# Expert slots of 64 rows in 16 rounds, or of 32 rows in 12 fixed passes: an encoder trunk with a sparse expert layer

## The chip, the cores and the metric

The kernel runs on one core of a Trainium2 chip. The time is the device time of one execution in microseconds, the median of several.

## The reference

Two layers work on 528 real positions (16 learned meta tokens and 512 frames) of 1024 features in float32. Layer 0 is multi-scale retention and then an expert layer; layer 1 is sliding-window attention with sinks and then an expert layer; a final norm follows. The diff touches only the expert layers:

```python
g_sel = argmax(softmax(t @ w_group))              # one of 4 groups
top_p, top_i = top_k(softmax(logits of the 4 experts in that group), 2)
weights = g_w * top_p / sum(top_p)
expert_idx = g_sel * 4 + top_i                    # 2 of 16 experts for each token
a, u = t @ w_gate[e], t @ w_up[e]                 # 1024 -> 256, each
y += (silu(a) * u * gate) @ w_down[e]             # 256 -> 1024
```

Gate and up weights of one expert are 2 MB, down weights 1 MB. Layer 0 routes 528 tokens, layer 1 512 (the meta tokens' outputs are no longer needed), each to two experts.

## The kernel before, in words

**Order of the stages.** Retention (up to about 540 us), expert layer 0, key/value/query projections and attention, expert layer 1, final norm. Each engine has its program written out by hand, with semaphores; nothing is planned by a scheduler. SP (SyncE) issues the loads of weights known beforehand, ACT (ScalarE) those of rows and the stores of results, POOL (GpSimd) the indirect transfers.

**Routing (DVE, L1436 to L1466).** PE's logits and a matmul with a triangular matrix give each token its rank within its expert. Each expert has a slot block of BLK = 64 rows; what is beyond is put into overflow blocks, of which there can be 16. DVE computes the slot of each token (`slot_i`, semaphore `slot_ready`) and then, for each overflow block, the rows of its expert's weights in DRAM (`w_row`, `eb_ready`). POOL scatters the normed tokens to `slot_rows` in DRAM (L1696, two transfers for a tile of tokens, ten in layer 0, eight in layer 1).

**Rounds.** A round works on 128 slot rows, two blocks of 64, each with its own expert. ACT loads the rows (`load_rows`, L1116), PE transposes them (L814, bank B_ROWS), DVE copies them with the gain, PE multiplies with gate and up weights (L828: 8 chunks of features, two halves of 64 columns, into one PSUM bank at partitions 0 and 64), ACT and DVE make the hidden values, PE transposes these (L835) and multiplies with the down weights (L849, banks B_YA and B_YB), ACT and DVE copy the result, ACT stores it to `slot_out`. PE's order is written out: gate/up k, hidden k-1, rows k+1, down k-1, then gate/up k+1. There are 8 rounds for the 16 experts' own blocks and 8 for the overflow blocks, whatever the routing.

**Weights.** Four buffers (`gu`, `down`) hold the weights of four blocks, so of two rounds. `first_weights` loads the first four during the stage before. SP's `experts` (L605) reloads the two buffers of round k when gate/up k-2 is done, and their down halves when down k-2 is done. From round 8 on POOL's `spilled` (L1700) does the same by indirect DMA, with the row indices from `w_row`: indices beyond a bound are skipped, so an unused overflow block loads only partition 0. POOL works this list strictly in order, waiting at each step.

**After the rounds** POOL gathers each token's two results (L1718) and DVE adds them, weighted, to the residual.

Of the kernel before, what the change touches and what calls it, by code (L numbers as in the profile page):

```python
# [32 lines left out]
BLK = 64  # L33
RING = 3
SLOTS_W = 4


def most_overflow(tokens):

    return max(m + min(m * ((tokens - BLK - 1) // BLK), (2 * tokens - (BLK + 1) * m) // BLK)  # L40
               for m in range(1, EXPERTS + 1) if (BLK + 1) * m <= 2 * tokens)


OVER = most_overflow(POS)
assert OVER % SLOTS_W == 0 == EXPERTS % SLOTS_W
THRESH = (POS - 1) // BLK
ROUNDS = (EXPERTS + OVER) // 2
SLOTS = 2 * ROUNDS * BLK
assert (EXPERTS + OVER) % 2 == 0 and ROUNDS % 2 == 0 and most_overflow(SEQ) <= OVER


C_ID, C_ONE, C_512, C_TRI = 0, 128, 256, 384
C_REV, C_THR, C_VALID, C_NH, C_EPS, C_FIRST, C_OVER, C_BLK, C_CAP, C_ROW = (
    512, 516, 524, 529, 534, 535, 551, 567, 583, 584)
NCONST = 586
# [4 lines left out]
def tables():  # L60
# [8 lines left out]
    c[:, C_THR:C_THR + THRESH] = np.arange(1, THRESH + 1) * BLK  # L69
    c[:, C_FIRST:C_FIRST + EXPERTS] = np.arange(EXPERTS) * BLK  # L70
    c[:, C_OVER:C_OVER + EXPERTS] = EXPERTS - 1 - np.arange(EXPERTS)
    c[:, C_BLK:C_BLK + OVER] = np.arange(OVER)
    c[:, C_CAP] = EXPERTS
    c[0, C_CAP] = EXPERTS - 1
# [106 lines left out]
def build(nc, a, out):  # L181
# [4 lines left out]
    with ctx:  # L186
# [21 lines left out]
        w_row = sb("w_row", [128, 2, OVER], I)  # L208
# [82 lines left out]
        down = cv(SLOTS_W, 2, D)  # L291
        gu_3 = cv(KT * 512)
        xg = cv(2, D)
        xgT = cv(2, KT, 128)
# [3 lines left out]
        lg = cv(5, 20)  # L298
        small = cv(1300)
        next_junk = cv(D)  # L300
        moe_junk = [arena[:, VALUES + KT * 512:VALUES + KT * 512 + D], arena[:, 15360:15360 + D]]
# [26 lines left out]
        slot_out = nc.dram_tensor("slot_out", (SLOTS, D), F).ap()  # L328
# [81 lines left out]
        def sigs(names, tag):  # L410
# [8 lines left out]
        gu_in, down_in, gu_over, down_over = ([sem(f"{n}{s}") for s in range(SLOTS_W)] for n in (  # L419
            "gate_up_in", "down_in", "gate_up_overflow_in", "down_overflow_in"))  # L420
# [10 lines left out]
        def gu(k):  # L431

            return gu_3 if k % SLOTS_W == 3 else ring[:, (k % SLOTS_W + 1) % RING]

# [5 lines left out]
        def weights_arrived(eng, given, spilled, l, k):  # L440

            if k < EXPERTS:
                eng.wait_ge(given[k % SLOTS_W], 16 * ((l * EXPERTS + k) // SLOTS_W + 1))
            else:
                eng.wait_ge(spilled[k % SLOTS_W], 16 * ((l * OVER + k - EXPERTS) // SLOTS_W + 1))

# [42 lines left out]
        sizes = dict(MASK=80, OV=80, T1=5, TOP=5, EQ=20, OHG=20, EG=20, G44=80, SEL=20, M1=5, M2=5, OH1=20, OH2=20, DX=5,  # L489
                     MA=80, MB=80, W1=5, W2=5, PRE=96, C5=16 * THRESH, NB=16, Z16=16, INCL=16, EB=16 * OVER, EBS=OVER,  # L490
                     BASE=16, SL=80, SF=10)
        ends = np.cumsum([0] + list(sizes.values())).tolist()
        (_, OV, T1, TOP, EQ, OHG, EG, G44, SEL, M1, M2, OH1, OH2, DX, MA, MB, W1, W2, PRE, C5, NB, Z16, INCL, EB, EBS,
         BASE, SL, SF) = ends[:-1]
# [6 lines left out]
        def gu_bank(k):  # L501
            return 2 + k % 2
# [13 lines left out]
        def in_pair(k):  # L516

            return 16 * (k // 2 + 1)
# [32 lines left out]
        def _(sp):  # L551
# [35 lines left out]
            def gate_up_weights(l, k):  # L587
                sp.dma_start(gu(k), a["w_gu"][l, k]).then_inc(gu_in[k % SLOTS_W], 16)

            def down_weights(l, k):  # L590
                sp.dma_start(flat(down[:, k % SLOTS_W]), a["w_down"][l, k])\
                    .then_inc(down_in[k % SLOTS_W], 16)

            def first_weights(l, readers):

                for k, used in enumerate(readers):
                    used()
                    gate_up_weights(l, k)
                    if k == 2:
                        down_weights(l, 0)  # L600
                        down_weights(l, 1)
                down_weights(l, 2)
                down_weights(l, 3)
# [10 lines left out]
            first_weights(0, (lambda: out_chunk_used(sp, 2), lambda: None,  # L614
                              lambda: out_chunk_used(sp, 3), lambda: None))
# [9 lines left out]
            for c in range(2):  # L625
# [5 lines left out]
                              lambda: fl.wait_full(sp, f"WO{NT - 1}"), lambda: None))  # L631
# [11 lines left out]
        def _(pe):  # L643
# [145 lines left out]
            def experts(l):  # L789
# [28 lines left out]
                def gate_up(k):  # L818
                    b = gu_bank(k)
                    for g in range(2):  # L820
                        weights_arrived(pe, gu_in, gu_over, l, 2 * k + g)
                    round_read(pe, l, B_ROWS, k)
                    if k >= 2:
                        round_read(pe, l, b, k - 2)
                    for c in range(KT):
                        for g in range(2):
# [12 lines left out]
                def down_project(k):  # L839
                    for g in range(2):  # L840
                        weights_arrived(pe, down_in, down_over, l, 2 * k + g)
                    round_read(pe, l, B_HID, k)
                    for n, b in enumerate((B_YA, B_YB)):
                        if k:
                            round_read(pe, l, b, k - 1)
                        for c in range(2):
                            for g in range(2):
                                half = slice(BLK * g, BLK * g + BLK)
                                last = mm(ps[half, b, :], hidT[:, c, half],  # L849
                                          down[:, (2 * k + g) % SLOTS_W, c, 512 * n:512 * n + 512],  # L850
                                          start=(c == 0), stop=(c == 1))
# [128 lines left out]
        def _(act):  # L980
# [114 lines left out]
            def experts(l, ready):  # L1095
# [15 lines left out]
                def load_rows(k):  # L1111

                    if k < ROUNDS:
                        if k >= 2:
                            round_full(act, l, B_ROWS, k - 2)
                        act.dma_start(xg[:, k % 2, :], slot_rows.rearrange("(b p) c -> b p c", p=2 * BLK)[k])\  # L1116
                            .then_inc(m[f"x_in{k % 2}"], 16)
# [5 lines left out]
                def results_of(k):  # L1123
# [3 lines left out]
                    if k >= 2:  # L1127
# [4 lines left out]
                    act.dma_start(slot_out.rearrange("(b p) c -> b p c", p=2 * BLK)[k], yo[:, j, :])\  # L1132
                        .then_inc(m[f"y_out{j}"], 16)
# [65 lines left out]
        def _(dve):  # L1199
# [158 lines left out]
            def experts(l):  # L1358
# [77 lines left out]
                step(V_.tensor_tensor(v(C5, 16, THRESH), count.unsqueeze(2).to_broadcast([128, 16, THRESH]),  # L1436
                                      con[:, C_THR:C_THR + THRESH].unsqueeze(1).to_broadcast([128, 16, THRESH]),
                                      ALU.is_gt))
                step(V_.tensor_reduce(v(NB, 16), v(C5, 16, THRESH), X, ALU.add))
                step(V_.memset(v(Z16, 16), 0.0))  # L1440
                step(V_.tensor_tensor_scan(v(INCL, 16), v(NB, 16), v(Z16, 16), 0.0, ALU.add, ALU.add))

                first = con[:, C_FIRST:C_FIRST + 16].unsqueeze(1).to_broadcast([128, nt, 16])
                step(V_.tensor_tensor(v(BASE, 16), v(INCL, 16), v(NB, 16), ALU.subtract))
                step(V_.tensor_tensor(v(BASE, 16), v(BASE, 16), con[:, C_OVER:C_OVER + 16], ALU.add))
                step(V_.tensor_scalar(v(BASE, 16), v(BASE, 16), float(BLK), None, ALU.mult))
                sl, over = v(SL, nt, 16), v(OV, nt, 16)
                V_.tensor_tensor(sl, ps[:, 2, 0:16 * nt].rearrange("p (t e) -> p t e", e=16), before[:, 0:nt, :],
                                 ALU.add).then_inc(free[2], 1)
                fl.wait_read(dve, f"RK{l}")  # L1450
                step(V_.scalar_tensor_tensor(over, sl, BLK - 0.5, v(BASE, 16).unsqueeze(1).to_broadcast([128, nt, 16]),
                                             ALU.is_gt, ALU.mult))
                step(V_.tensor_tensor(sl, sl, first, ALU.add))
                step(V_.tensor_tensor(sl, sl, over, ALU.add))
                for n, at in enumerate((MA, MB)):
                    step(V_.tensor_tensor(v(at, nt, 16), v(at, nt, 16), sl, ALU.mult))
                    step(V_.tensor_reduce(v(SF, 2, 5)[:, n, 0:nt], v(at, nt, 16), X, ALU.add))
                V_.tensor_copy(slot_i[:, :, 0:nt], v(SF, 2, 5)[:, :, 0:nt]).then_inc(m["slot_ready"], 1)
# [339 lines left out]
```

## Time and profile before

| | us |
|---|---|
| median of 3 runs | 1501.71 (1496.98 to 1505.82) |
| the profiled execution | 1498.73 |
| its span, first to last instruction | 1496.6 |
| PE busy | 1175.5 (79%) |
| PE weight loads (beside the matmuls) | 727.3 (49%) |
| DVE busy | 454.4 (30%) |
| POOL busy | 302.2 (20%) |
| ACT busy | 242.8 (16%) |
| mean granted TensorE clock | 0.888 |

Busy shares are means over stages with different limits. PE is nearly always busy during retention; in the two expert layers the DMA queues are the busiest for about half of each, and PE waits. The chain of waits and the instructions in order of time tell which it is at each place.

### The profile page before, as it was taken

How to read it: one execution, taken by the hardware profiler on the slowest of the kernel's cores; microseconds unless marked ns; L12 is line 12 of the kernel's file. 1: busy time of each engine (PE TensorE's matmuls, PEld its weight loads, DVE VectorE, ACT ScalarE, POOL GpSimd, SP SyncE). 2: the span in 40 equal slices, each digit the busy share in tenths (PEclk: the TensorE clock that was granted, in tenths of full speed). 3: DMA queues.
4: the chain of work that ended last, by engine and by line, in shares of the span. 5: the costliest groups of instructions: out<-in, count | busy, mean ns of one | idle time of the engine just before them, and what ended most of it. 6: DMA issues, size and time to landing. Idle time of an engine off the chain costs nothing.

```text
span 1496.6 us, 14033 instructions
## 1 busy us (share of the span) xinstructions
PE 1175.5 (79%) x5748; PEld 727.3 (49%) x5748; DVE 454.4 (30%) x736; ACT 242.8 (16%) x451; POOL 302.2 (20%) x232
## 2 busy tenths in 40 slices
PE   5999999999989982777779649688868296777790
PEld 4789698897967771322223224343434232322230
DVE  4212234322581033211112162635544311111114
ACT  4122221321421110000001010213213000000011
POOL 4133132231532202000222242100000200012124
PEclk9999999999999975988889959898988588998895
DMA  6141221321302353899995163100201769999825
GB/s 241 42 155 58 83 101 56 129 68 56 141 1 94 131 225 144 328 414 424 386 397 188 67 262 133 42 0 0 77 36 63 289 237 414 427 384 403 338 74 196
DMA packets 47176, 273.32 MB, mean 183 GB/s; under 512 B 8742, under 2 KB 8870, under 8 KB 33270
## 3 DMA queue, kind: packets, MB, share of 16 engines
q1 hardware_dynamic: 21168, 151.26, 25.7%
q0 software_dynamic: 13952, 77.15, 13.0%
q10 hardware_dynamic: 12000, 44.12, 7.4%
q8 instruction: 41, 0.67, 0.2%
q14 instruction: 15, 0.12, 0.0%
HBM read 277.28 MB, written 35.78 MB: 209 GB/s over the span
## 4 chain that ended last, share of the span: by engine, by line
PE 58%; issue 15%; DVE 11%; DMA 7%; POOL 6%; ACT 2%; ACTq 0%; POOLq 0%; SPq 0%; DVEq 0%
PE ps L665 19%; PE ps L828 14%; PE ps L849 6%; PE ps L886 4%; PE ps L972 4%; POOL ring_r L1672 4%; DMA ring<-in_w_gu,w_row 3%; PE ps L877 3%; DMA ring<-in_w_gu 2%; PE ps L814 2%; PE ps L798 2%; PE ps L751 2%; POOL slot_rows L1696 1%; DVE xT L1218 1%; DVE arena L1599 1%
## 5 line engine op out<-in xcount | busy, mean ns | idle before, releaser
L828 PE MATMUL ps<-ring,arena 128*64 128x512 f32 x768 | 258.4, 657 | 105.5 <-issue 99.5
L828 PEld LDWEIGHTS ps<-ring,arena 128*64 128x64 f32 x768 | 81.7, 151 | 272.9 <-issue 272.9
L665 PE MATMUL ps<-x_hi,ring_r 128*128 128x264 f32 x1024 | 190.9, 287 | 7.0 <-DVE xT_r L1206 7.0
L1672 POOL TENSOR_TENSOR ring_r<-ring,ring_r 128x1024 fp32r<-128x1024 f32 x56 | 134.2, 2408 | 301.5 <-ACT ring_r L999 301.5
L1218 DVE TENSOR_TENSOR arena<-ps,gains 128x512 f32<-128x512 f32 (+1 forms) x74 | 46.7, 673 | 397.8 <-PE ps L814 384.1
L665 PE MATMUL ps<-ring_r,x_hi 128*128 128x512 f32 (+1 forms) x480 | 155.8, 406 | 11.6 <-POOL ring_r L1672 11.6
L665 PEld LDWEIGHTS ps<-x_hi,ring_r 128*128 128x128 f32 x1024 | 160.3, 189 | 7.5 <-DVE xT_r L1206 7.3
L665 PE MATMUL ps<-xT_r,ring_r 128*128 128x264 f32 x512 | 146.1, 285 | 0.0
L828 PE MATMUL ps<-arena 128*64 128x512 f32 x256 | 133.9, 683 | 0.0
L849 PE MATMUL ps<-arena 128*64 128x512 f32 x512 | 116.9, 598 | 4.3 <-ACT arena L1121 4.3
L665 PEld LDWEIGHTS ps<-ring_r,x_hi 128*128 128x128 f32 (+1 forms) x480 | 84.3, 176 | 43.3 <-POOL ring_r L1672 13.1
L665 PEld LDWEIGHTS ps<-xT_r,ring_r 128*128 128x128 f32 x512 | 97.0, 189 | 0.1
L999 ACT ACTIVATE ring_r<-ring 128x1024 fp32r<-128x1024 f32 x56 | 57.7, 1052 | 123.1 <-PE ps L665 73.7
L1121 ACT ACTIVATE arena<-ps 128x256 f32<-128x256 f32 x32 | 12.3, 383 | 388.3 <-PE ps L835 383.8
L1702 POOL DMA_INDIRECT arena<-in_w_down,w_row x32 | 31.6, 988 | 202.7 <-PE ps L849 197.8
L1702 POOL DMA_INDIRECT ring<-in_w_gu,w_row x24 | 23.9, 995 | 240.7 <-PE ps L828 234.0
L814 PE MATMUL ps<-con,arena 128*128 128x128 f32 x256 | 35.1, 283 | 46.3 <-DMA arena<-slot_rows 46.3
L886 PE MATMUL ps<-ring,xT 128*128 128x512 f32 x128 | 59.8, 628 | 10.2 <-DVE arena L1599 10.2
L849 PEld LDWEIGHTS ps<-arena 128*64 128x64 f32 x512 | 34.7, 136 | 64.0 <-issue 64.0
L665 PE MATMUL ps<-ring_r,xT_r 128*128 128x512 f32 (+1 forms) x160 | 65.0, 406 | 0.0
L1660 POOL TENSOR_SCALAR var<-ss 128x1 f32<-128x1 f32 (+1 forms) x23 | 9.0, 391 | 259.8 <-ACT arena L987 259.3
L653 PE MATMUL ps<-con,arena 128*128 128x128 f32 (+1 forms) x152 | 24.1, 320 | 41.1 <-DVE arena L1212 39.3
(177 smaller groups left out, 1494.9 us busy)
## 6 DMA issues: line engine op xcount, KB each, us to landing
ring<-in_w_gu SPq DMA_DIRECT2D x24, 2048.0 KB, 14.1
arena<-in_w_down SPq DMA_DIRECT2D x32, 1024.0 KB, 10.4
ring<-in_w_ret SPq DMA_DIRECT2D x48, 512.0 KB, 3.6
arena<-in_w_gu SPq DMA_DIRECT2D x8, 2048.0 KB, 19.1
arena<-slot_rows ACTq DMA_DIRECT2D x32, 512.0 KB, 7.3
slot_out<-arena ACTq DMA_DIRECT2D x32, 512.0 KB
slot_rows<-arena ACTq DMA_DIRECT2D x8, 1024.0 KB, 4.0
ring<-in_w_ret_out SPq DMA_DIRECT2D x16, 512.0 KB, 4.5
```

What stands on the lines that cost most here:

```text
L665: last = mm(dst, a_parts[x], b_parts[y], start=(start and n == 0), stop=(stop and n == 2))
L751: last = mm(ps[:, b + g, c - lo:HALF], v_tm[0:r, t, 128 * m:128 * m + 128], scores_of(t)[0:r, c - 128 * t:hi - 128 * t], start=(t == 0), s ...
L814: last = nc.tensor.transpose(ps[:, c // 4, 128 * (c % 4):128 * (c % 4) + 128], xg[:, k % 2, 128 * c:128 * c + 128], ident)
L828: last = mm(ps[half, b, :], xgT[:, k % 2, c, half], by_row(gu(2 * k + g))[:, c, :], start=(c == 0), stop=(c == KT - 1))
L849: last = mm(ps[half, b, :], hidT[:, c, half], down[:, (2 * k + g) % SLOTS_W, c, 512 * n:512 * n + 512], start=(c == 0), stop=(c == 1))
L877: last = mm(ps[0:rows(t), b, :], xTk[:, k, col0(t):col0(t) + rows(t)], w_kv[:, k, :], start=(k == 0), stop=(k == KT - 1))
L886: last = mm(ps[:, b, :], xT[:, k, col0(t):col0(t) + 128], w_q[c][:, k, :], start=(k == 0), stop=(k == KT - 1))
L972: last = mm(ps[:, 4 + c, :], oT1[:, k, :], w[:, k, :], start=(k == 0), stop=(k == KT - 1))
L999: nc.scalar.activation(w_hi[to][:, m], w_raw[slot][:, m], ACT.Copy).then_inc(hi_made, 1)
L1218: return V_.tensor_tensor(dst[:, 4 * g:4 * g + 4, c0:c0 + r], src, gains[:, gain, 4 * g:4 * g + 4].unsqueeze(2).to_broadcast([128, 4, r]), ...
L1672: G.tensor_tensor(w_lo[slot][:, m], w_raw[slot][:, m], w_hi[to][:, m], ALU.subtract).then_inc(lo_made, 1)
L1702: return G.indirect_dma_start(dst, None, w.rearrange("l e p c -> (l e p) c"), bass.IndirectOffsetOnAxis(w_row[:, l, k - EXPERTS:k - EXPERT ...
```

## The change

Slots are counted in tiles of 32 rows. An expert with n tokens has ceil(n/32) tiles, taken two at a time as *pairs* (called doubles, "d", 64 rows) and the rest as *singles* ("s", 32 rows); there are 16 pair places and 16 single places. Single place j has no weights of its own: it shares the weight buffer of pair place j, and an expert's odd tile goes to the single beside its own pair where it has one. The passes are a fixed list of 12. A pass has 128 columns: two pairs, a pair and two singles, or four singles. With two singles in a half, gate/up and down have three matmuls for each chunk in place of two, with 64, 32 and 32 columns; with four singles, four.

The ring of weight buffers has six places (W_SLOTS). The first five experts are loaded ahead (AHEAD) in order of number. When the routing is known POOL goes over them (`others`, with `mended`) and loads another expert where the pair place has one; for the same expert all indices but that of partition 0 are out of bounds. From the sixth on SP loads with an address taken from the register of the expert's number. Before a pass with singles POOL goes over the two buffers once more (`reload`, with `gu_again` and `down_again`), which loads another expert if the single's is not the pair's, and only partition 0 if it is. PE waits for these in `weights_arrived`. Rows and results of a pass go in two transfers of 64 rows. DVE's routing is written anew.

```diff
-RING = 3
-SLOTS_W = 4
+TILE = 32
+W_SLOTS = 6
+AHEAD = 5
+PASSES = [(("d", 0), ("d", 1)), (("d", 2), ("s", 0)), (("d", 3), ("d", 4)), (("s", 2), ("d", 5)),
+          (("d", 6), ("s", 4)), (("d", 7), ("d", 8)), (("s", 6), ("d", 9)), (("d", 10), ("s", 8)),
+          (("d", 11), ("d", 12)), (("s", 10), ("d", 13)), (("d", 14), ("d", 15)), (("s", 12), ("s", 14))]
...
+        def column_tiles(k):
+            for n, (kind, j) in enumerate(PASSES[k]):
+                if kind == "d":
+                    yield slice(BLK * n, BLK * n + BLK), j
+                else:
+                    for g in range(2):
+                        yield slice(BLK * n + TILE * g, BLK * n + TILE * g + TILE), j + g
...
+        def weights_arrived(eng, first, again, l, k):
+            for kind, j in PASSES[k]:
+                if kind == "d":
+                    double_arrived(eng, first, l, j)
+                else:
+                    singles_arrived(eng, again, l, j)
...
             def experts(l):
-                for k in range(2, EXPERTS // 2):
-                    round_full(sp, l, gu_bank(k), k - 2)
-                    for g in range(2):
-                        gate_up_weights(l, 2 * k + g)
-                    round_full(sp, l, B_YB, k - 2)
-                    for g in range(2):
-                        down_weights(l, 2 * k + g)
+                m = mo[l]
+                sp.wait_ge(m["eb_ready"], 1)
+                for j in range(AHEAD, EXPERTS):
+                    if j < W_SLOTS:
+                        sp.wait_ge(m["scattered"], 16 * 2 * (5 - l))
+                    e = sp.value_load(e_of[0:1, l, j:j + 1], min_val=0, max_val=EXPERTS - 1)
+                    gu_d, dn_d = a["w_gu"][l], a["w_down"][l]
+                    if j >= W_SLOTS:
+                        round_full(sp, l, gu_bank(pass_of("s", j - W_SLOTS)), pass_of("s", j - W_SLOTS))
+                    gate_up_weights(l, j, gu_d[bass.ds(e, 1)].rearrange("a p c -> p (a c)"))
+                    if j >= W_SLOTS:
+                        round_full(sp, l, B_YB, pass_of("s", j - W_SLOTS))
+                    down_weights(l, j, dn_d[bass.ds(e, 1)].rearrange("a p c -> p (a c)"))
...
                     for c in range(KT):
-                        for g in range(2):
-                            half = slice(BLK * g, BLK * g + BLK)
-                            last = mm(ps[half, b, :], xgT[:, k % 2, c, half], by_row(gu(2 * k + g))[:, c, :],
+                        for cols, j in column_tiles(k):
+                            last = mm(ps[cols, b, :], xgT[:, k % 2, c, cols], by_row(gu(j))[:, c, :],
                                       start=(c == 0), stop=(c == KT - 1))
...
-                for k in range(EXPERTS // 2, ROUNDS):
-                    round_full(pool, l, gu_bank(k), k - 2)
-                    for n in (2 * k, 2 * k + 1):
-                        spilled(a["w_gu"], gu(n), n).then_inc(gu_over[n % SLOTS_W], 16)
-                    round_full(pool, l, B_YB, k - 2)
-                    for n in (2 * k, 2 * k + 1):
-                        spilled(a["w_down"], flat(down[:, n % SLOTS_W]), n).then_inc(down_over[n % SLOTS_W], 16)
+                for j in range(AHEAD):
+                    pool.wait_ge(gu_in[j % W_SLOTS], times_filled(l, j))
+                    others(a["w_gu"], gu(j), j).then_inc(mended[j // 2 > 0], 16)
+                    pool.wait_ge(down_in[j % W_SLOTS], times_filled(l, j))
+                    others(a["w_down"], flat(down[j % W_SLOTS]), j).then_inc(mended[j // 2 > 0], 16)
+
+                def reload(w, dst, arrived, k):
+                    for n in range(0, EXPERTS, 2):
+                        if pass_of("d", n + 1) == k:
+                            for j in (n, n + 1):
+                                others(w, dst(j), AHEAD + j).then_inc(arrived[n // 2 % 2], 16)
+
+                for k in range(ROUNDS):
+                    round_full(pool, l, gu_bank(k), k)
+                    reload(a["w_gu"], gu, gu_again, k)
+                    round_full(pool, l, B_YB, k)
+                    reload(a["w_down"], lambda j: flat(down[j % W_SLOTS]), down_again, k)
```

## Rows read from the trace of the kernel before

**Rows 1.** DMA rate (GB/s) in 40 slices of 8 us from 560 us.

```profile
GB/s 0 110 371 191 2 163 428 282 437 420 429 395 414 421 431 426 405 434 424 433 292 379 419 425 431 290 433 407 437 127 225 112 70 72 68 39 92 195 344 4
```

**Rows 2.** Chain that ended last, both expert stages (start us, us, what).

```profile
593.46 9.72 PE ps L828 x32
605.68 7.09 PE ps L828 x32
...
728.17 13.03 DMA ring<-in_w_gu,w_row
...
834.05 6.87 PE ps L828 x32
...
841.96 3.67 PE ps L849 x16
...
847.44 3.67 PE ps L849 x16
...
1201.36 9.56 PE ps L828 x32
...
1457.29 3.67 PE ps L849 x16
```

**Rows 3.** The page's DMA queues: packets, MB, share of 16 engines.

```profile
q0 software_dynamic: 13952, 77.15, 13.0%
```

**Rows 4.** PE in order of time, rounds of layer 0 (start us, us, line, operands [idle before]).

```profile
655.91 8.78 PE L828 MATMUL ps<-ring,arena 128*64 128x512 f32 x32 [3.01 <-issue]
795.31 3.65 PE L849 MATMUL ps<-arena 128*64 128x512 f32 x16
798.80 7.04 PE L828 MATMUL ps<-ring,arena 128*64 128x512 f32 x32
806.04 1.04 PE L814 MATMUL ps<-con,arena 128*128 128x128 f32 x8
807.01 3.65 PE L849 MATMUL ps<-arena 128*64 128x512 f32 x16
```

**Rows 5.** PE in order of time, single matmuls of L828.

```profile
606.57 0.59 PE L828 MATMUL ps<-ring,arena 128*64 128x512 f32 x1
606.60 0.59 PE L828 MATMUL ps<-arena 128*64 128x512 f32 x1
606.99 0.59 PE L828 MATMUL ps<-ring,arena 128*64 128x512 f32 x1
```

**Rows 6.** PE and its weight loads (PEld) at 453 us, L665.

```profile
453.05 0.39 PE L665 MATMUL ps<-ring_r,y_lo 128*16 128x512 f32 x1
453.27 0.39 PE L665 MATMUL ps<-w_hi_b,y_hi_b 128*128 128x512 f32 x1
453.05 0.19 PEld L665 LDWEIGHTS ps<-w_hi_b,y_hi_b 128*128 128x128 f32 x1
```

**Rows 7.** POOL in order of time, scatter and indirect loads.

```profile
583.36 0.84 POOL L1696 DMA_INDIRECT slot_rows<-arena,slot_i  x1 [0.30 <-issue]
799.77 0.99 POOL L1702 DMA_INDIRECT arena<-in_w_down,w_row  x1 [18.62 <-PE ps L849]
```

**Rows 8.** DMA issues: KB each, median us to landing; first 560 to 880, then 810 to 846.

```profile
arena<-slot_rows ACTq DMA_DIRECT2D x16, 512.0 KB, 7.3
...
arena<-slot_rows ACTq DMA_DIRECT2D x1, 512.0 KB, 3.3
...
ring<-in_w_gu,w_row POOLq DMA_INDIRECT x3, 3.1
```

**Rows 9.** DVE in order of time, routing of layer 0.

```profile
567.55 0.29 DVE L1436 TENSOR_TENSOR arena<-arena,con 128x128 f32<-128x128 f32 x1
...
570.02 0.24 DVE L1454 TENSOR_TENSOR arena<-arena 128x80 f32<-128x80 f32 x1
...
571.40 0.17 DVE L1458 CAST slot_i<-arena 128x10 int32<-128x10 f32 x1
571.48 0.42 DVE L1461 TENSOR_TENSOR arena<-arena,con 128x256 f32<-128x256 f32 x1
```

More of the change, by code:

```diff
@@ L290, in build @@
         cv = Carve()
[L291 to L294, printed above, removed]
+        gu_arena = cv(2, KT * 512)
+        down = [*(lambda d: [d[:, n] for n in range(AHEAD)])(cv(AHEAD, 2, D))]
         yo = cv(2, D)
@@ L846, in down_project @@
                         for c in range(2):
[L847 to L850, printed above, removed]
+                            for cols, j in column_tiles(k):
+                                last = mm(ps[cols, b, :], hidT[:, c, cols], down[j % W_SLOTS][:, c, 512 * n:512 * n + 512],
                                           start=(c == 0), stop=(c == 1))
@@ L1443, in experts @@
[L1443 to L1448, printed above, removed]
-                                 ALU.add).then_inc(free[2], 1)
@@ new lines, in experts @@
+                pos = v(POSN, nt, 16)
+                V_.tensor_tensor(pos, ps[:, 2, 0:16 * nt].rearrange("p (t e) -> p t e", e=16), before[:, 0:nt, :],
+                                 ALU.add).then_inc(free[2], 1)
+                step.done(V_.tensor_reduce(v(N_, 16), passed, X, ALU.add))
+                step.done(V_.memset(v(Z16, 16), 0.0))
+                step(V_.tensor_reduce(v(D_, 16), passed[:, :, 1:THRESH:2], X, ALU.add))
+                P0, P1 = v(PP, 17)[:, 0:16], v(PP, 17)[:, 1:17]
@@ new lines, in experts @@
+                step.done(V_.tensor_tensor(v(PC, nt, 16), pos, per_expert(v(CC, 16)), ALU.add))
+                step(V_.tensor_tensor(v(DBL, nt, 16), v(DBL, nt, 16), per_expert(v(CA, 16)), ALU.mult))
+                step(V_.tensor_tensor(v(PC, nt, 16), v(PC, nt, 16), v(DBL, nt, 16), ALU.add))
+                for at in (MA, MB):
+                    step.done(V_.tensor_tensor(v(at, nt, 16), v(at, nt, 16), v(PC, nt, 16), ALU.mult))
+                step.wait()
+                place = v(SLOT, 2, 5)
@@ new lines, in experts @@
+                step(V_.tensor_reduce(eo, match, X, ALU.add))
+                step.done(V_.tensor_scalar(v(FREE, 16), v(CL, 16), -1.0, 1.0, ALU.mult, ALU.add))
+                step(V_.tensor_scalar(eo, eo, float(EXPERTS - 1), None, ALU.min))
+                step.done(V_.tensor_copy(e_of[:, l, :], eo))
+                step.done(V_.tensor_copy(to[:, 0:AHEAD], eo[:, 0:AHEAD]))
+                step.done(V_.tensor_tensor(same[:, 0:AHEAD], eo[:, 0:AHEAD], num[:, 0:AHEAD], ALU.is_equal))
+                step.done(V_.tensor_tensor(dif, xo, num, ALU.add))
@@ new lines, in experts @@
+                step.wait()
+                step(V_.tensor_tensor(match, v(IL, 16).unsqueeze(1).to_broadcast([128, 16, 16]), c16(dif, 16), ALU.is_le))
+                step(V_.tensor_reduce(xo, match, X, ALU.add))
+                step.done(V_.tensor_tensor(dif, xo, eo, ALU.subtract))
+                step(V_.scalar_tensor_tensor(v(PM, 16), xo, float(EXPERTS), v(FREE, 16), ALU.is_lt, ALU.mult))
+                step(V_.tensor_tensor(dif, dif, v(PM, 16), ALU.mult))
+                step.done(V_.tensor_tensor(to[:, AHEAD:], eo, dif, ALU.add))
@@ L1468, in widen @@
+                step(V_.tensor_scalar(same[:, AHEAD:], dif, 0.0, None, ALU.is_equal))
+                step(V_.tensor_scalar(same, same, con[:, C_FAR:C_FAR + 1], con[:, C_ROW:C_ROW + 1], ALU.mult, ALU.add))
+                step(V_.scalar_tensor_tensor(to, to, 128.0, same, ALU.mult, ALU.add))
+                V_.tensor_scalar(w_row[:, l, :], to, float(128 * EXPERTS * l), None, ALU.add).then_inc(m["eb_ready"], 1)
                 def widen(k):
```

227 lines of the change are left out of this document (142 added, 85 removed).

## The prediction

> **What bounds the kernel now.** I read the page's busy shares first (PE 79%, nothing else over 30%), then its 40 slices, which show that DMA is nearly full only in the two expert stages, then the DMA rate inside them [rows 1], then the chain of waits in them [rows 2] and last the engines' own order of time. The reader is to see three phases in each expert stage (586 to 852 and 1194 to 1462 us). Rounds 2 to 7 wait for DMA: the ten slices from 632 to 712 us move 423 GB/s on average, and I take 420 for a full DMA [rows 1]. Rounds 8 to 12, the overflow rounds, wait for the indirect loads that POOL issues only when the round two before is done (the piece `ring<-in_w_gu,w_row` [rows 2]). Rounds 13 to 15 load next to nothing and run at PE's own pace. The expert part proper is 593.46 to 851.11 us in layer 0 and 1201.36 to 1460.96 in layer 1 (first L828 to the end of the last L849) [rows 2]: 257.7 and 259.6 us. Everything outside is a different stage that the diff leaves alone, but for the routing on DVE.
>
> **What the routing of this input is.** From the reference's inputs I counted the tokens of each expert: in both layers every expert has between 41 and 84, so each has one block of 64, and 9 of them in layer 0 and 10 in layer 1 one overflow block. The trace agrees: 19 spilled experts of 3.146 MB, 8.5 MB of scatter and 8.5 MB of gather, and row 0 of the 13 unused blocks make 77.1 MB, and q0 moved 77.15 [rows 3]. In the new scheme each expert therefore has one pair (j = e), and its third tile of 32, if any, is the single that shares its buffer. Nothing is mended or reloaded but partition 0. So the second load of 19 experts, 59.8 MB, goes; 142 us at 420 GB/s is an upper bound of what that alone could give. 16 rounds become 12 passes per layer.
>
> **PE's own time.** At full pace a round is 11.69 us: L828 starts at 798.80, L849 at 795.31 and again at 807.01, 11.70 later [rows 4]. An instruction streams 512 columns in 0.43 us, and the two halves of 64 columns run together: starts 0.03 us apart, the next two 0.43 later [rows 5]. A pass of two pairs is the same work. Six passes (1, 3, 4, 6, 7, 9) have a pair and two singles, three instructions in a step instead of two, and the last has four. A pass has 16 such steps in gate/up and 8 in down. The trace has no step of three tiles in different column groups. Bounds: 0.43 us, if all overlap (L814 and its loads issue 16 instructions in 1.04 us [rows 4], 0.065 each, so six loads and matmuls fit in 0.39); 0.86 us if tiles of 64 and of 32 columns take turns; 1.18 us, two whole instructions of 0.59, if the array also empties between them. I take 0.43: the nearest row is the change from 16 columns to 128 at 453 us, where the load for 128 starts with the last 16-column matmul (453.05) and its matmul 0.22 us later, the ordinary spacing, before the 0.39 of the last is over [rows 6]. There nothing empties. These two use the same columns, so the row doesn't show that different widths overlap; that stays the largest risk.
>
> The Trainium skill says the opposite for the emptying: "Mode switching requires drain", a change of tile shape drains TensorE (TensorEngine Tiling (Array Packing), Tiling Modes). By that rule the step is the 1.18 us case, and the trace disagrees with it for 16 against 128 columns. No row here shows it for 64 against 32.
>
> **The sum for one layer, first L828 to last L849.**
> Undisturbed: first to second L828 12.2 us (593.46 to 605.68), ten more passes of 11.69, and 17.0 from the last L828 to the end (834.05 to 851.11) [rows 2, 4]: 146.1.
>
> New waits. Every single's buffer now waits for an indirect load by POOL, though it carries only partition 0. POOL takes them strictly in order: gate/up of pass k, reload, *down of pass k*, reload. PE starts gate/up k+2 right after down k. So the reload of gate/up for a single in pass k+2 is issued only when down k has ended, with nothing of PE's left beside it. Price: POOL starts 0.81 us after down ends (798.96 to 799.77), the second load 1.29 later (0.99 and the 0.30 between two issues) [rows 4, 7], and a load of only row 0 lands 3.1 us after its issue where DMA is quiet [rows 8]: 5.2, and 5.4 with PE's head start of 0.16 (798.96 to 798.80). That is for passes 3, 6, 9. In passes 4, 7, 11 two down loads stand ahead on POOL, 2.6 more: 8.0. Pass 1 waits for the reload after gate/up 0: 603.18 + 0.8 + 1.29 + 3.1 = 608.4 against 605.7, 2.7. Down of the last pass waits for the reload behind down 10: 5.2 against a natural gap of 1.8 (845.6 to 847.44, [rows 2]), 3.4. Together 2.7 + 3 x 5.4 + 3 x 8.0 + 3.4 = 46.3.
>
> Contention. At passes 3, 6, 7 and 9 SP's weight loads are in flight. Row loads land in 7.3 us in the whole stage against 3.3 alone [rows 8]; twice as many bytes in time explains about one of the four, so I add 3 each, 12 (bounds 0 and 4 x 8).
>
> Clock. After an idle gap of 3.01 us the next gate/up took 8.78 us instead of 7.04 [rows 4], and after the long idle time before 593.46 9.72 [rows 2]: PE's clock stood at its lower level (1.2 GHz) for the first steps. The stalls here are a little longer than 3.01, so six at 1.9: 11.4.
>
> DMA as the limit. After the five experts loaded ahead 11 x 3.146 = 34.6 MB remain, with 12.6 MB of rows and results: 112 us at 420 GB/s. By buffers: the weights of 10 are issued after down 3, some 10 us behind those of 8 and 9, and are due at pass 7; those of 15 are issued after down 7, behind 12.6 MB since down 6, and land some 25 us after down 6, where pass 10 starts at 23.4 plus one stall. Everything is just in time, so I charge nothing.
>
> Loads and rows of the first passes: two experts' checks (four POOL issues, 5.2 us) follow the scatters and start at 583.36 + 0.84 + 0.3, the fourth at 588.4, and land at 591.5, before L828 at 593.5 [rows 7]: nothing. The six issues of the other three experts take 7.7 us more and land before pass 1. The fifth expert loaded ahead adds 3.1 MB, 7.5 us, to a queue that was empty before the scatter [rows 1]: nothing. SP's reading of the expert number stands before a wait that ends later: nothing.
>
> Routing on DVE. From L1436 to the end of L1458 4.0 us for 16 instructions; an instruction of 10 or 16 columns takes 0.17 us, of 80 0.24, of 256 0.42, and a dependent one starts 0.04 later [rows 9]. The new list up to slot_ready has 3.2 us of the first size (12 waits at 0.21, and what is issued between them at 0.08), 2.0 of 80 columns and 3.4 of 160 to 272: 8.6 us. +4.6, on the path, since the scatter waits for it. The list after it is longer, but lies beside 12.5 us of scatters.
>
> Stage: 146.1 + 46.3 + 12 + 11.4 = 215.8. Gains 257.7 - 215.8 - 4.6 = 37.3 and 259.6 - 215.8 - 4.6 = 39.2: 76.5. The profiled execution took 1498.7 (span 1496.6), 3.0 under the median 1501.7, so 1498.7 - 76.5 + 3.0 = 1425.
>
> **The rivals.**
> *A, the forecast*, 1425. Bounds within it: no contention and half the clock loss give 18 us a layer more, 1389; contention of 8 us at four passes 20 less, 1465.
> *B, the widths take turns, slower.* In a pair-and-singles pass steps of 64 and of 32 columns do not overlap: 0.43 us more in 24 steps of 6 passes, 62 us a layer. It decides from a step of 0.43 + 76.5/288 = 0.70 us on. For: [rows 5] show overlap only of equal widths. Against: [rows 6]. Time: 1425 + 124, less some 15 of contention that the slower pace removes, 1534.
> *C, they also empty the array.* 0.75 more, 216 in all: 1626. Against: [rows 6] again, and more plainly. This is what the Trainium skill's rule above would do here.
> *D, three tiles overlap, but the third adds its own issue*: L814's load and matmul take 0.13 us each (8 in 1.04 [rows 4]), a step 0.56: 288 x 0.13 = 37, 1462.
> *E, it doesn't do what it says*: experts are reloaded after all (another count in a tile at a threshold). 3.1 MB, 7.5 us at 420 GB/s, on the path per expert: two of them 1440. Against: the number of pairs changes only below 33 and above 96 tokens, and the counts are 41 to 84.
> *F, the waits on POOL are free*, if reloads land before PE needs them: 46 + 12 + 11 a layer less, 1287. Against: POOL's order.
>
> **Chances.** A 0.50, D 0.14, B 0.17, C 0.10, E 0.03, F 0.06. The range takes in A, D and B with their bounds and leaves out C and F: 1370 to 1550. Beside it, the likeliest's own: 1389 to 1465. About 0.5% (7.5 us) is what a measurement of this kernel tells from no change. Faster: A, D, E and F, less 0.02 for the upper end of D: 0.71. Same: those 0.02 and 0.01 of B's lower end. Slower: the rest of B, and C, 0.26.
>
> **What would show it.** L828's instructions in pass 3 start three together with 0.43 us between steps (B: 0.86, C: 1.18). Gate/up stands idle 5 to 12 us before passes 3, 4, 6, 7, 9, 11 and not before 2, 5, 8, 10, each time with a POOL load just ahead, not SP's. q0 moves about 18 MB, not 77. slot_ready comes 8 to 9 us after the compare. Wrong would be: gaps before passes 2, 5, 8 (then DMA is late), or busy time of L828 per pass over 9 us at full clock.

## The result and the profile after

The changed kernel takes 1704.8 us (median, 1700.1 to 1707.7) against 1501.7: ratio 1.135, 95% interval 1.130 to 1.140. It is 203 us slower where 77 us faster was forecast, and beyond the stated range.

| | before | after |
|---|---|---|
| profiled execution's span, us | 1496.6 | 1705.1 |
| q0 moved, MB | 77.15 | 18.12 |
| DMA packets under 512 B | 8742 | 16940 |
| first L828 (now L893) to last L849 (now L912), layer 0 | 257.7 | 348.1 |
| the same, layer 1 | 259.6 | 348.9 |

The bytes did what the prediction said. This is the page's queue after, for [rows 3]:

```profile
q0 software_dynamic: 16832, 18.12, 3.2%
```

The chain of waits in expert layer 0, after, for [rows 2] (start us, us, what; x48 is the gate/up of a pass with a pair and two singles, x32 of one with two pairs):

```profile
592.90 13.20 DMA arena<-in_w_down,w_row
606.35 9.94 PE ps L893 x32
618.35 3.51 DMA ring<-in_w_gu,w_row
622.10 17.52 PE ps L893 x48
...
644.45 6.87 PE ps L893 x32
652.56 7.96 PE ps L912 x24
662.64 12.90 DMA arena<-in_w_gu,w_row
675.58 18.20 PE ps L893 x48
695.02 3.58 PE ps L912 x16
698.61 8.76 issue
707.37 17.68 PE ps L893 x48
726.29 7.51 PE ps L912 x23
734.23 6.87 PE ps L893 x31
742.34 10.65 issue
753.00 10.77 PE ps L912 x24
...
944.28 3.74 DMA arena<-in_w_down,w_row
948.11 6.29 PE ps L912 x32
```

Two things are to be seen. A mixed gate/up takes 17.5 to 18.2 us where a plain one takes 6.87, and a mixed down 7.5 to 8.0 instead of 3.6: PE itself is slow. And PE stands idle before passes 3, 4 and down 4, for 15.1, 8.8 and 10.7 us. Ahead of pass 3 the chain names a load that carries `w_row`, so one of POOL's; ahead of pass 4 and down 4 it names no releaser ("issue"), and that these are POOL's loads too is shown only by e_noreload below. PE's waits for weights in this stage, grouped (us in total, times, longest):

```profile
PE ps L893 <- DMA arena<-in_w_gu,w_row: 30.0, 2, 15.1
PE ps L893 <- issue: 25.2, 3, 8.8
PE ps L912 <- issue: 21.2, 2, 10.7
PE ps L893 <- DMA ring<-in_w_gu,w_row: 20.1, 2, 15.3
PE ps L893 <- DMA arena<-in_w_down,w_row: 8.5, 1, 8.5
PE ps L912 <- DMA arena<-in_w_down,w_row: 5.5, 1, 5.5
```

That is 110.5 us, 102.0 of it after the first L893. PE in pass 4, in order of time, for [rows 5]:

```profile
716.06 1.05 PE L893 MATMUL ps<-arena,xT 128*32 128x512 f32 x4
717.04 1.07 PE L893 MATMUL ps<-ring,xT 128*64 128x512 f32 x2
718.04 1.05 PE L893 MATMUL ps<-arena,xT 128*32 128x512 f32 x4
```

A chunk has six instructions: the 64 column tile twice, one after the other, and then each of the two 32 column tiles twice, these two together. From 32 to 64 columns and back to 32 is 1.98 us (716.06 to 718.04). Four streams of 0.43 one after the other would be 1.72; so the widths do not overlap, and each of the two changes of width in a chunk costs 0.13. In pass 11, where all four tiles have 32 columns, they do overlap, all four within 0.02 us, and the next four start 0.43 later:

```profile
934.74 0.61 PE L893 MATMUL ps<-ring,xT 128*32 128x512 f32 x3
934.76 0.59 PE L893 MATMUL ps<-arena,xT 128*32 128x512 f32 x1
935.16 0.61 PE L893 MATMUL ps<-ring,xT 128*32 128x512 f32 x3
```

### The profile page after: what moved, and what is told of

It is laid out like the page before. It is cut to its first block, busy times and chain, and to the rows that moved or that the text cites. A ratio compares the mean times of both kernels' runs of the same rounds, so it can differ in the third digit from the quotient of the medians.

```text
span 1705.1 us, 14072 instructions
## 1 busy us (share of the span) xinstructions
PE 1259.8 (74%) x5668; PEld 694.0 (41%) x5668; DVE 448.4 (26%) x785; ACT 232.8 (14%) x427; POOL 322.0 (19%) x252
## 2 busy tenths in 40 slices
DMA packets 48521, 205.91 MB, mean 121 GB/s; under 512 B 16940, under 2 KB 17068, under 8 KB 39420
## 3 DMA queue, kind: packets, MB, share of 16 engines
q0 software_dynamic: 16832, 18.12, 3.2%
## 4 chain that ended last, share of the span: by engine, by line
PE 58%; issue 18%; DMA 8%; DVE 8%; POOL 6%; ACT 1%; POOLq 0%; ACTq 0%; DVEq 0%
PE ps L893 18%; PE ps L732 16%; PE ps L912 9%; PE ps L948 4%; PE ps L1034 4%; POOL ring_r L1799 3%; DMA arena<-in_w_gu,w_row 3%; PE ps L939 2%; DMA ring<-in_w_gu,w_row 2%; PE ps L818 1%; DMA arena<-in_w_down,w_row 1%; PE ps L881 1%; DVE arena L1726 1%; DVE arena L1729 1%; POOL slot_rows L1823 1%
## 5 line engine op out<-in xcount | busy, mean ns | idle before, releaser
L893 PE MATMUL ps<-ring,xT 128*64 128x512 f32 (+1 forms) x576 | 214.6, 686 | 113.7 <-DMA ring<-in_w_gu,w_row 40.1
L893 PE MATMUL ps<-arena,xT 128*64 128x512 f32 (+1 forms) x448 | 191.6, 662 | 46.3 <-DMA arena<-in_w_gu,w_row 29.8
L912 PE MATMUL ps<-arena 128*64 128x512 f32 (+1 forms) x512 | 153.8, 674 | 54.9 <-issue 42.4
L1282 DVE TENSOR_TENSOR xT<-ps,gains 128x512 f32<-128x512 f32 (+1 forms) x84 | 51.7, 661 | 485.2 <-PE ps L881 482.6
L893 PEld LDWEIGHTS ps<-ring,xT 128*64 128x64 f32 (+1 forms) x576 | 44.3, 135 | 271.8 <-issue 207.6
L1829 POOL DMA_INDIRECT arena<-in_w_down,w_row x42 | 41.5, 989 | 456.5 <-PE ps L912 412.1
L732 PEld LDWEIGHTS ps<-ring_r,x_hi 128*128 128x128 f32 (+1 forms) x480 | 84.3, 176 | 43.3 <-POOL ring_r L1799 13.1
L912 PEld LDWEIGHTS ps<-arena 128*64 128x64 f32 (+1 forms) x512 | 31.1, 132 | 160.6 <-issue 160.6
L893 PEld LDWEIGHTS ps<-arena,xT 128*64 128x64 f32 (+1 forms) x448 | 36.9, 129 | 132.7 <-issue 101.0
L881 PE MATMUL ps<-con,xT 128*128 128x128 f32 x192 | 26.8, 286 | 64.2 <-DMA xT<-slot_rows 64.2
L1615 DVE COPY arena<-ps 128x512 f32<-128x512 f32 x24 | 16.6, 692 | 162.6 <-PE ps L912 162.6
```

The lines of the kernel that those rows point to most:

```text
L732: last = mm(dst, a_parts[x], b_parts[y], start=(start and n == 0), stop=(stop and n == 2))
L881: last = nc.tensor.transpose(ps[:, c // 4, 128 * (c % 4):128 * (c % 4) + 128], xg[:, k % 2, 128 * c:128 * c + 128], ident)
L893: last = mm(ps[cols, b, :], xgT[:, k % 2, c, cols], by_row(gu(j))[:, c, :], start=(c == 0), stop=(c == KT - 1))
L912: last = mm(ps[cols, b, :], hidT[:, c, cols], down[j % W_SLOTS][:, c, 512 * n:512 * n + 512], start=(c == 0), stop=(c == 1))
L1282: return V_.tensor_tensor(dst[:, 4 * g:4 * g + 4, c0:c0 + r], src, gains[:, gain, 4 * g:4 * g + 4].unsqueeze(2).to_broadcast([128, 4, r]), ...
L1829: return G.indirect_dma_start(dst, None, w.rearrange("l e p c -> (l e p) c"), bass.IndirectOffsetOnAxis(w_row[:, l, n:n + 1], 0), bounds_c ...
```

## The experiments

The two costs were taken apart: the width of the tiles on PE, and the loads of POOL's second look. All times are medians; the ratio is to the kernel before on the same chip. Beside these runs the kernel before had medians of 1501.1 to 1507.8 us, so a difference between two runs below is good to some 7 us.

| run | us | ratio, 95% interval |
|---|---|---|
| the change | 1704.8 | 1.135 (1.130 to 1.140) |
| e_split | 1546.7 | 1.025 (1.021 to 1.030) |
| e_noreload | 1452.8 | 0.963 (0.959 to 0.967) |
| e_split_noreload | 1350.7 | 0.894 (0.891 to 0.898) |
| e_grouped | 1678.6 | 1.113 (1.108 to 1.117) |
| e_tworow | 1620.1 | 1.080 (1.075 to 1.085) |
| e_poolorder | 1570.7 | 1.045 (1.042 to 1.049) |
| e_spwait | 1633.7 | 1.086 (1.082 to 1.091) |
| b_mixed | 1794.7 | 1.192 (1.187 to 1.197) |
| b_all32 | 1508.6 | 1.002 (0.999 to 1.005) |
| e_split_poolorder | 1446.6 | 0.962 (0.958 to 0.966) |
| e_best | 1341.3 | 0.890 (0.886 to 0.895) |

**e_split: one width in a pass.**

```diff
-                if kind == "d":
+                if kind == "d" and all(w == "d" for w, _ in PASSES[k]):
                     yield slice(BLK * n, BLK * n + BLK), j
+                elif kind == "d":
+                    for g in range(2):
+                        yield slice(BLK * n + TILE * g, BLK * n + TILE * g + TILE), j
```

> The changed kernel, but in passes with singles the pair is multiplied as two tiles of 32 columns with the same weights, so all tiles of a step have one width. Theory 1 (tiles of 64 and of 32 columns never run together and each change of width costs 0.13 us): gate/up of a mixed pass falls from 17.5 to about 7 us, down from 7.5 to 3.7, so 12 passes x 14.4 = 173 us less, about 1532 us, and up to 1570 if POOL's and SP's loads are late instead. Theory 2 (it is the third tile as such, its instruction or its weight stream, that costs): four tiles a step are no faster than three, 1705 us or more.

158 us less. The mixed passes now issue more instructions, 64 in a gate/up where there were 48, and take about half the time: in layer 0 the six gate/ups 54.6 us together where they took 106.6, their downs 26.1 where they took 53.3. Theory 2 is out. The 15 us that are missing to 173 are not in waits, which are as long as before (109.9 us in layer 0, 110.5 in the changed kernel); they are the clock. Each mixed gate/up still stands behind a gap and begins at the lower clock level, so it takes 8.5 to 9.9 us and not the 7 of theory 1.

**e_noreload: no second look.** `reload` in POOL and `singles_arrived` in PE are left out; they brought partition 0 of the same expert again.

> The changed kernel without POOL's second look at the buffers (reload) and without PE's wait for it; with this input they carry only partition 0, which is the same data. Theory 1 (the gaps before passes 3, 4, 6, 7, 9, 11 and before down 4, 7 and 11 are these loads stuck behind SP's weights): all gaps go, some 95 us a layer, about 1500 us. Theory 2 (DMA is late anyway, SP's weights would end these gaps at the same time): only the part that stood in quiet DMA goes, 8 + 8 + 8 us a layer, about 1655 us.

252 us less, more than theory 1 had; theory 2 is out. Most of the 50 us beyond its 200 is PE's clock, which I had not counted in the 95 us a layer: the gaps and the steps at the lower level behind them go together. Here is the expert stage of layer 0 in the changed kernel and in this one (window, its length, busy us of PE, PEld, DVE, ACT, POOL with instructions in brackets, granted clock, DMA share, GB/s):

```profile
606.00:953.00 347.00, 243.88 (x872) 59.39 (x876) 30.88 (x57) 15.18 (x36) 31.63 (x32) 0.82 0.37 125
```

```profile
600.00:833.00 233.00, 219.61 (x884) 56.74 (x882) 32.83 (x60) 15.18 (x36) 0.29 (x1) 0.98 0.55 190
```

The granted clock is 0.98 against 0.82, and PE is busy 24 us less on the same instructions, beside some 100 us less of standing still (347.00 - 243.88 = 103.1 against 13.4, of which some 10 lie in the window but outside the stage).

**e_split_noreload: both.**

> Both edits: one width in a pass, and no reload (partition 0 is the same data). Theory 1 (PE's taking turns and the reload are all that costs, and they add up): 12 passes of 11.7 us, 1705 - 173 - 200 = 1330 us. Theory 2 (with both gone SP's weights are the limit: 34.6 MB a layer in a ring of six whose places come free late): gaps before passes 5 to 10 with SP's loads ahead of them, 1380 us or more.

1350.7. Together they give 354 us where alone they give 158 and 252 (410): the split is worth 102 once the reloads are gone. In layer 0 the windows are 233 us above and 184 here (they begin 7 and 9 us ahead of the first gate/up):

```profile
600.00:784.00 184.00, 148.59 (x1024) 52.31 (x1024) 31.78 (x59) 15.18 (x36) 1.98 (x2) 0.92 0.71 244
```

PE is busy 71 us less (219.61 - 148.59), and 22 of them come back as idle time (13.4 becomes 35.4). Its largest waits there, and the places of them in the chain (start us, us, what):

```profile
PE ps L894 <- issue: 16.3, 2, 11.3
PE ps L894 <- DMA arena<-in_w_down,w_row: 10.2, 1, 10.2
```

```profile
681.76 7.07 PE ps L894 x64
...
704.00 3.57 PE ps L913 x32
707.57 11.30 issue
718.86 8.66 PE ps L894 x32
```

x64, a mixed gate/up, takes 7.07 us. 10.2 is the first look. For the 11.30, the gap before pass 8, the chain names no releaser, but the trace of SP's loads does. Pass 8 needs the gate/up weights of expert 12; SP issues that load at 689.04, when gate/up 6 has ended (KB, us from issue to landing):

```profile
ring<-in_w_gu SPq DMA_DIRECT2D x1, 2048.0 KB, 29.7
```

It lands at 718.74, and gate/up 8 begins at 718.86. The other gap of the 16.3, 4.96 us before pass 10, ends in the same way: the load for expert 15 is issued at 733.62, takes 15.3 us, and pass 10 begins at 748.98. DMA is full around them: from 640 to 730 us its engines are busy 96% of the time and 30.59 MB arrive, 340 GB/s on average. So theory 2's limit by SP's weights is there, in small size (1350.7 us, between the 1330 and the 1380 of the two theories).

**e_grouped: 64 column tiles first, then those of 32.**

```diff
-                    for c in range(KT):
-                        for cols, j in column_tiles(k):
+                    for width, c in [(w, c) for w in (BLK, TILE) for c in range(KT)]:
+                        for cols, j in [x for x in column_tiles(k) if x[0].stop - x[0].start == width]:
```

> The changed kernel with the tiles of a mixed pass in another order: all chunks of the 64 column tile, then all chunks of the two 32 column tiles; same instructions. Theory 1 (widths take turns at 0.43 us a step each, and a change of width costs 0.13 us): seven chunks' changes go in gate/up (1.9 us) and three in down's two banks together with (0.8 us), 12 x 2.7 = 32 us less, 1673 us. Theory 2 (the cost is a full emptying of the array, 0.16 us or more beyond, at each change): over 50 us less. Theory 3 (order does nothing, each tile simply costs its stream): 1705 us.

26 us less, 32 by theory 1. The widths still take turns, only with fewer changes. Theory 1 counted one thing too many: in a down the new order leaves out four changes (seven become three), not six, so 0.13 us a change gives 28 us and not 32. A mixed down at full clock shows it alone: 7.94 us in the changed kernel, 7.40 here, 0.13 for each of the four. Its pass 4 (PE in order of time):

```profile
701.10 9.63 PE L893 MATMUL ps<-ring,xT 128*64 128x512 f32 x16 [8.31 <-issue]
710.67 7.06 PE L893 MATMUL ps<-arena,xT 128*32 128x512 f32 x32
```

The 32 narrow instructions, 16 pairs, take 7.06, as 16 pairs of 64 columns do in [rows 4]. The 16 wide ones begin at the lower clock level.

**b_mixed and b_all32: the width alone, in the kernel before.** Each round multiplies the same two blocks, cut otherwise:

```diff
-                        for g in range(2):
-                            half = slice(BLK * g, BLK * g + BLK)
+                        for half, g in COLS:
+# b_mixed: COLS = [(slice(0, 64), 0), (slice(64, 96), 1), (slice(96, 128), 1)]
+# b_all32: COLS = [(slice(32 * q, 32 * q + 32), q // 2) for q in range(4)]
```

> The kernel before with one edit: the second half of every round is multiplied as two tiles of 32 columns with the same weights, the first stays one of 64. Nothing of slots, loads or POOL changes. Theory 1 (widths take turns, 0.13 us for each change): every gate/up takes about 16 us in place of 7 and every down 7.5 in place of 3.7; where DMA paces the rounds (2 to 7) 7 us a round show, elsewhere up to 13: 120 to 150 us a layer, 1740 to 1800 us. Theory 2 (what was slow in the changed kernel was its weights of three experts in a step, three streams): here the streams of a step are three as well but of two buffers; if that matters, less than 60 us in all.

> The kernel before, with both halves as two tiles of 32 columns each, so four instructions in a step where there were two and one width throughout. Theory 1 (tiles of one width run together, up to four): within 0.5% of before, 1500 us. Theory 2 (the number of instructions or of streams costs): 0.1 us and more a step, 24 steps in 32 rounds, over 60 us slower.

1794.7 and 1508.6. The mixture alone costs 290 us (1504.9 for the kernel before beside these runs); four tiles of one width cost nothing that can be measured. Theory 1 holds in both. The chunk of b_mixed is that of the changed kernel (1.98 us from 32 to 32), with only two weight buffers:

```profile
820.55 1.05 PE L828 MATMUL ps<-arena 128*32 128x512 f32 x4
821.54 1.07 PE L828 MATMUL ps<-ring,arena 128*64 128x512 f32 x2
822.54 1.05 PE L828 MATMUL ps<-arena 128*32 128x512 f32 x4
```

**e_poolorder: POOL in PE's order.**

```diff
                     reload(a["w_gu"], gu, gu_again, k)
-                    round_full(pool, l, B_YB, k)
-                    reload(a["w_down"], lambda j: flat(down[j % W_SLOTS]), down_again, k)
+                    if k:
+                        round_full(pool, l, B_YB, k - 1)
+                        reload(a["w_down"], lambda j: flat(down[j % W_SLOTS]), down_again, k - 1)
```

> The changed kernel, but POOL reloads gate/up for the next singles before it waits for the down of the pass before (PE's own order). Theory 1 (POOL's order is what exposes them): they are issued 8 to 11 us earlier, in quiet DMA, and land while PE does that down; the gaps before passes 3, 4, 6, 7, 9, 11 go (15 + 9 + 15 + 8 + 15 + 8 = 70 us a layer, and some clock loss), those before down 4, 7 and 11 stay: 1545 us. Theory 2 (the wait moves to SP's weights or to the same semaphores of the down halves): half of it, about 1620 us.

134 us less, 160 expected: POOL's order was a little over half of the 252 us that e_noreload gives. The gaps before passes 3, 6, 9 and 11 go. Before passes 4 and 7, where theory 1 had none, gaps of 7.78 and 7.88 us stay, some 31 us if layer 1 has the same. Before pass 4 POOL issues the reload at 678.54, when gate/up 3 has ended, and SP waits for the same event and issues its 2 MB at 677.85.

**e_tworow and e_spwait: why a load of one partition lands so late.** The first lists 2 partitions in place of 128 in every indirect weight load (`dst[0:2]`, `w_row[0:2, ...]`); the second lets SP issue its weights only when POOL's reload of that moment has landed (`singles_arrived(sp, ...)` after `round_full(sp, l, B_YB, p)`).

> The changed kernel, but every indirect weight load (the first look and the reloads) lists 2 partitions in place of 128; the 126 skipped ones are left out, partition 0 is loaded as before (for a routing in which an expert moves it would be incomplete). Theory 1 (each skipped partition is a small transfer that takes its turn between SP's 16 KB ones, so 256 to 512 of them hold up a reload for 13 us): reloads land 3 to 4 us after their issue also beside SP's loads; 9 us less at passes 3, 6, 9 and downs 4, 7, and 8 less before pass 0, 53 us a layer, about 1600 us. Theory 2 (a small load simply waits until SP's bytes queued before it have moved): same gaps, 1700 us.

> The changed kernel, but SP issues its weights for two experts only after POOL's reload that is due at the same moment has landed. Theory 1 (a reload is slow only beside SP's loads): it lands 4 us after its issue in place of 13; gaps before 3, 6, 9 shrink by 9 each and those before downs 4 and 7 go, 49 us a layer, about 1607 us. Theory 2 (the loads that SP now issues later are themselves due): the gaps turn up before passes 5, 7 or 10 instead, 1680 us or more.

85 and 71 us less, of 105 and 98. In both the waits before downs 4 and 7 all but go (21.2 us in the changed kernel, 3.5 in e_tworow). The same load, the one before pass 3, in the chains of e_tworow and of e_spwait (start us, us from issue to landing), beside 12.90 above:

```profile
658.04 8.09 DMA arena<-in_w_gu,w_row
```

```profile
666.12 4.26 DMA arena<-in_w_gu,w_row
```

With 126 skipped partitions less it is 4.8 us faster, but not at the 3 to 4 us of theory 1; without SP's weights beside it, and with all 128 listed, it is 8.6 faster. So both theories hold in part. The same loads before passes 6 and 9 took 13.1 and 12.7 us in the changed kernel. In e_tworow they take 6.5 and 6.8, so there the skipped entries were worth 6 us and more. In e_spwait they take 11.4 and 9.9: the loads of SP that its edit holds back meet the next reload instead. POOL issues the one of pass 6 at 748.0, and a load of 2 MB that SP issued at 738.21 lands only at 758.8, half a microsecond before it. So e_spwait stays short of its 98 us. Where DMA is quiet the skipped entries cost little: the loads before pass 1 and before the last down land in 3.51 and 3.74 us in the changed kernel and in 3.44 and 3.14 in e_tworow. The page's count of packets under 512 B shows the entries: 8742 before, 16940 after, 7532 in e_tworow. The Trainium skill says that each DMA engine takes turns between its queues packet by packet (DMA: Bandwidth & Descriptors, Queues, rings and completion order); that entries which move nothing cost 4.8 us and more beside SP's loads, and at most 0.6 in quiet DMA, agrees with that.

**e_split_poolorder and e_best: towards a better kernel.** The second has both edits and a branch; POOL reads partition 1 of `w_row`, which tells whether another expert is wanted:

```diff
+                def if_other(n, loads):
+                    v = pool.value_load(w_row[1:2, l, n:n + 1], min_val=0, max_val=16384)
+                    with pool.If(v < 2 * 128 * EXPERTS):
+                        for w, dst, arrived in loads:
+                            others(w, dst, n).then_inc(arrived, 16)
+                    with pool.Else():
+                        for w, dst, arrived in loads:
+                            pool.sem_inc(arrived, 16)
```

> The changed kernel with the pairs of mixed passes as two tiles of 32 columns and with POOL's reloads in PE's order. Theory 1 (both costs are separate): 1547 less some 110 (the gaps before passes 3, 4, 6, 7, 9, 11 in it; PE's downs are shorter now and cover less of a reload): 1440 us. Theory 2 (with PE so fast the reloads are exposed again wherever SP is loading): 1490 us.

> As the run before, and POOL reads for each weight load whether another expert is wanted and issues it only then (otherwise it raises the semaphore itself); right for any routing. Theory 1 (the loads that carry nothing new are the rest of the cost): as without reloads, 1350 us, and some 15 less for the first look: 1340. Theory 2 (reading a register and branching costs POOL some us each time): 1380 to 1400 us.

1446.6 and 1341.3: theory 1 in both, to 7 us and to 1 us. POOL's branches are not to be seen. The kernel beats that before by 11% (ratio 0.890), keeps the 12 passes, and issues the extra loads only where another expert is wanted. With this routing none is, so the branch that issues them never ran; how the kernel does with an uneven routing was not measured. Its largest wait in layer 0 (600 to 775 us) is again for SP's weights: 9.95 us before pass 8, whose load of 2 MB is issued at 681.87 and lands 28.3 us later, at 710.17; the gate/up begins at 710.27. In PE's waits (us in total, times, longest):

```profile
PE ps L896 <- issue: 13.9, 3, 10.0
```

## Why the prediction was wrong

In layer 0 it came out 140 us too low: 132 in the stage (348.1 against 215.8) and 8 ahead of it. The 132 are, worked out from the traces, some 80 for the widths, 40 for waits on POOL's loads and 12 for the clock. By its own steps:

**"I take 0.43": the step that failed.** The cost of a step with two widths was bounded by 0.43, 0.86 and 1.18 us and taken at the lower end. It is 0.99. Gate/up of passes 1, 3, 4, 6, 7 and 9 is 106.6 us together (6 x 7.04 = 42.2 foreseen), their downs 53.3 (21.9 foreseen). Part of that is the clock behind the gaps. At full clock, in e_noreload, a mixed gate/up takes 15.7 us and a mixed down 7.9, so the widths cost 0.56 us in each of 144 steps, 80 us a layer. b_mixed and b_all32 show it alone. B was the right mechanism (0.86), with a price for each change that it didn't have. C's total was a third too high, because it let every step change the width: PE changes twice in a chunk of two steps, not four times. C's price of 0.16 (0.59 - 0.43) for each of two changes would make a chunk of 2.04 us, where 1.98 was measured, so B and C are closer to each other here than they were made to look. The value came from [rows 6], where a 16 column tile is followed by one of 128 columns at the ordinary spacing. That row is true and says that nothing empties there; but its two tiles use the same columns and could not have overlapped. It spoke against C and was let speak against B. The text named this as the largest risk and still gave B 0.17. The Trainium skill's rule, that a change of tile shape drains TensorE (TensorEngine Tiling (Array Packing), Tiling Modes), was nearer to the truth than my reading: tiles of 64 and 32 columns run apart here, and a change costs 0.13 us, a little less than the 0.16 that I had for emptying the array.

**The waits on POOL: mechanism right, size not.** They stood where they were forecast: passes 3, 4, 6, 7, 9, 11, none before 2, 5, 8, 10. In quiet DMA the price held: 8.76, 8.29 and 8.20 us at passes 4, 7 and 11 against 8.0, and 4.81 at pass 1, 3.3 over the gap of 1.5 before, where 2.7 was foreseen. At passes 3, 6 and 9 it was 15.1, 15.3 and 14.9 against 5.4 + 3. The term that was mis-sized is the contention, 3 us each: it is 9.5 to 9.9 us, from SP's bytes and from the skipped partitions. At pass 7, where 3 were charged too, there is none. I read it from row loads, which are dense, and took an indirect load of one partition for a small thing.

**Downs 4 and 7: missed.** They waited 10.65 and 10.54 us for their down reload. The working let a down reload land in 5.6 us, beside 8 us of gate/up. It was issued with SP's weights, and took longer than that: with two entries listed (e_tworow) the two waits are 1.8 and 1.7 us.

**The first look, "nothing".** L893 began at 606.35, 8.3 us after the 598.1 that the routing alone gives. The four loads land 13.2 us after the last issue, beside SP's sixth expert and the rows, which move 3.8 MB in that time; the working had 3.1 us. With the skipped entries left out they land after 7.75 us, and e_tworow starts 4.4 us earlier, at 601.94.

**The clock: right where it was charged, and not charged everywhere.** The six mixed gate/ups lose 12.3 us (106.6 against 6 x 15.7), for 11.4. Downs 4 and 7 and both halves of the last pass also begin at the lower level and lose 10.8 more, the first gate/up 1.0: together 24 us a layer, the same 24 by which PE is less busy in e_noreload.

**Right:** the routing (first compare to slot_ready 8.75 us for 8.6; first scatter at 576.24, 4.36 later than before, for 4.6), q0's 18 MB, and that no weights of SP's are late in the changed kernel. They only appear as a limit when PE and POOL are mended. One reading was off without effect: the ten slices from 632 to 712 us have a mean of 420 GB/s, not 423; the working used 420.

The forecast's gain was real: e_best has it, and 84 us more than forecast, since it does without the waits on POOL (rival F's mechanism, 1287). That it comes so near F is no credit to the forecast: F had 0.06, and against it stood POOL's order, which e_best changes.

## What to carry to other kernels

When tiles of different widths are to share a step on TensorE, don't argue from rows where they follow each other in the same columns: ask for a row where both are free to run, and without one price the mixture as taking turns. Cutting the wide tile into narrow ones of one width costs nothing here and gives the overlap. A load that is skipped almost wholly isn't free: beside whatever SP issues at the same event it lands four times as late as alone (12.9 us for 3.1 here), so put it in PE's order, or branch around it.

## What the runs showed of the hardware

- Tiles of 128x64 and 128x32 in different column groups do not overlap in float32: 1.98 us a chunk where four streams one after another are 1.72, so 0.13 us for each change of width (a down with four changes less: 7.40 us for 7.94). Two tiles of 64 or four of 32 do: 0.43 us a step.
- Four instructions and four weight loads in a step of 0.43 us are no limit (b_all32, ratio 1.002).
- An indirect load of which 127 of 128 partitions are skipped lands 3.1 to 3.8 us after its issue in quiet DMA, 12.7 to 13.1 beside direct loads (4.2 MB in one case), and 6.5 to 8.1 beside them with only 2 partitions listed.
- A register read and a branch on POOL ahead of each possible weight load cost nothing to be seen: e_best takes 1341.3 us where e_split_noreload takes 1350.7. The second pays for the first look besides, whose absence lets e_best's first gate/up of layer 0 begin 6.6 us earlier; with that taken off in both layers (an estimate, 1337.5) some 4 us are left for all branches together.
